# Expert weights of a mixture-of-experts trunk: loads of two units at a time, with a permuted inner index

## What is computed

```
def ffn(args):
    xb, e = args
    return (jax.nn.silu(xb @ w1[e]) * (xb @ w3[e])) @ w2[e]
```

## Time and profile before

| | |
|---|---|
| median of 3 runs | 2397.04 us (2386.5 to 2398.64) |
| the profiled execution | 2395.54 us |
| its span in the trace | 2393.7 us |
| PE busy | 2203.8 us, 92% |
| DVE busy | 1577.6 us, 66% |
| ACT busy | 1243.1 us, 52% |
| bytes moved by DMA | 598.04 MB, mean 250 GB/s |

### The profile page before, as it was taken

How to read it: one execution, slowest core, us unless ns; L and a number is a source line. 1 busy time by engine, 2 the same in 40 slices (tenths; PEclk the granted TensorE clock), 3 DMA queues, 4 the chain that set the end, 5 groups by cost and what they waited for, 6 DMA issues and landing times.

```text
span 2393.7 us, 30553 instructions
## 1 busy us (share of the span) xinstructions
PE 2203.8 (92%) x11545; PEld 1825.2 (76%) x11545; DVE 1577.6 (66%) x1338; ACT 1243.1 (52%) x1007; POOL 96.2 (4%) x74
## 2 busy tenths in 40 slices
PE   4798889999999999899897899999999999999991
PEld 3776667888999999688786777777777777777771
DVE  5433332443545455544535799999999999999996
ACT  2322223443333232233422588888888888888870
POOL 1000000000000000000100000000000000000000
PEclk9977777999999999899998799999999999999995
DMA  4411213565544444355644299999999999999983
GB/s 157 145 62 62 66 54 103 189 204 164 185 159 159 157 159 146 100 192 193 213 141 181 110 416 411 406 421 412 420 412 419 408 419 409 416 405 421 410 347 143
DMA packets 153498, 598.04 MB, mean 250 GB/s; under 512 B 15648, under 2 KB 19856, under 8 KB 102080
## 3 DMA queue, kind: packets, MB, share of 16 engines
q1 hardware_dynamic: 149760, 589.60, 64.8%
q0 software_dynamic: 3680, 7.64, 1.0%
HBM read 590.90 MB, written 18.87 MB: 255 GB/s over the span
## 4 chain that ended last, share of the span: by engine, by line
PE 72%; DVE 14%; issue 9%; ACT 2%; DMA 1%; POOL 0%; DVEq 0%; SPq 0%; ACTq 0%; POOLq 0%
PE ps L1488 19%; PE ps L1474 13%; PE ps L864 9%; DVE wl L618 8%; PE ps L865 8%; PE ps L861 5%; PE ps L845 3%; PE ps L886 2%; PE ps L1536 2%; PE ps L1557 1%; PE ps L1580 1%; PE ps L1578 1%; ACT wh L507 1%; PE ps L1548 1%; DVE yall L743 1%
## 5 line engine op out<-in xcount | busy, mean ns | idle before, releaser
L618 DVE TENSOR_TENSOR wl<-raw,wh 128x2048 fp32r<-128x2048 f32 x352 | 786.8, 2287 | 58.7 <-ACT wh L507 57.5
L507 ACT ACTIVATE wh<-raw 128x2048 fp32r<-128x2048 f32 x352 | 665.0, 1913 | 122.6 <-PE ps L865 73.4
L1168 DVE TENSOR_TENSOR wl<-raw,wh 128x2048 fp32r<-128x2048 f32 x161 | 368.9, 2292 | 498.2 <-ACT wh L1028 498.2
L1028 ACT ACTIVATE wh<-raw 128x2048 fp32r<-128x2048 f32 x161 | 308.1, 1914 | 631.9 <-PE ps L1488 301.2
L864 PE MATMUL ps<-wh,xg 128*128 128x512 f32 x900 | 383.5, 426 | 0.9 <-issue 0.7
L865 PE MATMUL ps<-wl,xg 128*128 128x512 f32 x900 | 360.6, 401 | 0.0
L1474 PE MATMUL ps<-hth,wh 128*128 128x272 f32 (+1 forms) x896 | 261.2, 291 | 15.4 <-DVE wl L1168 9.9
L1474 PE MATMUL ps<-htl,wh 128*128 128x272 f32 (+1 forms) x896 | 258.6, 289 | 0.0
L1474 PE MATMUL ps<-hth,wl 128*128 128x272 f32 (+1 forms) x896 | 258.2, 288 | 0.0
L864 PEld LDWEIGHTS ps<-wh,xg 128*128 128x128 f32 x900 | 173.9, 193 | 52.6 <-DVE wl L618 9.7
L864 PE MATMUL ps<-wh,hx 128*128 128x512 f32 x508 | 204.9, 403 | 3.4 <-DVE hx L736 3.4
(11 more groups left out here) (320 smaller groups left out, 3227.3 us busy)
## 6 DMA issues: line engine op xcount, KB each, us to landing
raw<-in_w_dram SPq DMA_DIRECT2D x384, 1024.0 KB, 8.2
raw<-in_w_in_dram SPq DMA_DIRECT2D x104, 1024.0 KB, 5.1
raw<-in_w_pa_dram SPq DMA_DIRECT2D x16, 1024.0 KB, 5.0
raw<-in_w_pb_dram SPq DMA_DIRECT2D x16, 1024.0 KB, 5.0
raw<-in_w_out_dram SPq DMA_DIRECT2D x16, 1024.0 KB, 5.1
raw<-in_w_ukv_dram SPq DMA_DIRECT2D x8, 1024.0 KB, 5.3
raw<-in_w_uq_dram SPq DMA_DIRECT2D x8, 768.0 KB, 4.5
yrow<-yscr SPq DMA_DIRECT2D x4, 1024.0 KB, 10.8
```

What stands on the lines that cost most here:

```text
L507: nc.scalar.activation(wh2[:, x % HELD, :], raw2[:, slot2(x), :], ACT.Copy).then_inc(s_wh2, 1)
L618: nc.vector.tensor_tensor(wl2[:, slot2(x), :], raw2[:, slot2(x), :], wh2[:, x % HELD, :].bitcast(F32), ALU.subtract).then_inc(s_wl2, 1)
L1028: nc.scalar.activation(wh[:, n % 2, :], raw1[:, n % RING1, :], ACT.Copy).then_inc(s_wh, 1)
L1168: nc.vector.tensor_tensor(wl[:, n % 2, :], raw1[:, n % RING1, :], wh[:, n % 2, :].bitcast(F32), ALU.subtract).then_inc(s_wl, 1)
```

## The change

Two neighbouring units, in two neighbouring slots, are loaded by one DMA of 2 MB, 16 KB in one run per partition. A matrix is two loads instead of four. A load waits until both slots are used (`x + 1 - RING2`), and both units share one semaphore, so there are four instead of eight; `hi` and `unit` wait on the semaphore of the pair of slots. `landed2` keeps its values.

`w2` is now viewed as `w1` is: partition p has the rows 4 p to 4 p + 3, and unit c has row 4 p + c. So the hidden index is permuted: the 128 hidden values of unit c are those at 4 p + c. ACT's copy to `ab` makes that order, by reading PSUM with a step of 4 elements; `mix` reads `ab[:, v, f, :]`.

```
-        ab = place("ab", [P, 2, FF], M0)
+        ab = place("ab", [P, 2, KF, P], M0)
-        s_raw2 = [sem(f"s_raw2_{i}") for i in range(RING2)]
+        s_raw2 = [sem(f"s_raw2_{i}") for i in range(RING2 // 2)]
...
                 else:
-                    done(sp, turn, x - RING2)
-                sp.dma_start(unit_view(raw2, slot2(x)) if len(src.shape) == 3 else raw2[:, slot2(x), :],
-                             src).then_inc(s_raw2[slot2(x)], 16)
+                    done(sp, turn, x + 1 - RING2)
+                s = slot2(x)
+                sp.dma_start(raw2[:, s:s + 2, :].rearrange("p s u -> p (s u)"), src).then_inc(s_raw2[s // 2], 16)
+
+            def matrix(turn, x, w, e):
+
+                v = w[bass.ds(e, 1), :, :].rearrange("a (p k) n -> p (a k n)", p=P)
+                for h in range(2):
+                    load(turn, x + 2 * h, v[:, 2 * U * h:2 * U * (h + 1)])
             def up(turn, x, w, e):
-                v = w[bass.ds(e, 1), :, :].rearrange("a (p k) n -> p (a k) n", p=P)
-                for u in range(4):
-                    load(turn, x + u, v[:, 4 * u:4 * u + 4, :])
+                matrix(turn, x, w, e)
             def down(turn, x, e):
-                for c in range(KF):
-                    load(turn, x + c, w2[bass.ds(e, 1), P * c:P * (c + 1), :].rearrange("a p n -> p (a n)"))
+                matrix(turn, x, w2, e)
...
-                act.wait_ge(s_raw2[slot2(x)], landed2(turn, x))
+                act.wait_ge(s_raw2[slot2(x) // 2], landed2(turn, x))
...
-                nc.scalar.activation(ab[:, v, :], ps[:, v, :], ACT.Copy).then_inc((s_ac, s_bc)[v], 1)
+                nc.scalar.activation(ab[:, v, :, :], ps[:, v, :].rearrange("q (p c) -> q c p", c=KF), ACT.Copy).then_inc((s_ac, s_bc)[v], 1)
...
-                    pe.wait_ge(s_raw2[slot2(x)], landed2(turn, x))
+                    pe.wait_ge(s_raw2[slot2(x) // 2], landed2(turn, x))
...
-                        nc.tensor.matmul(ps[:, 6, c:c + SLOTS], ab[:, v, P * f:P * (f + 1)], fold[:, :],
+                        nc.tensor.matmul(ps[:, 6, c:c + SLOTS], ab[:, v, f, :], fold[:, :],
```

## The result

The changed kernel takes 2460.5 us (median of 6 runs, 2453.2 to 2466.3), the kernel before 2395.2 us in the same runs: a ratio of 1.028, with a 95% interval from 1.025 to 1.031. The forecast was 2403 us, with a range from 2387 to 2420. The change is slower by 65 us, more than ten times the 6 us that the sum had.

The account below looks back on a forecast made before the run. PE was taken to bound half of each pair of experts and DVE the other half, with DMA close. 15 pairs x 0.4 us = 6 us, on top of 2397.0 us, gave 2403 us, with a range from 2387 to 2420.

Parts of the forecast that it names:

- What bounds the kernel now: Expert stage: four resources within a few per cent; PE bounds half of each pair of experts, DVE the other; 61.4 us average.
- Fewer, longer loads: Expert weight loads: 16 KB runs take 2.43 instead of 2.48 us per MB, 1.2 us of 60 per pair.
- The copy to `ab` and the order of `w2`: ACT's stepped PSUM read, 587 ns to double, taken at nothing; the hidden index's order, nothing.
- The ring in pairs: Expert-stage loads: the even unit lands 2.5 us later, costing 0.4 us per pair, with 0 and 1.2 as ends.
- I take its late landings at nothing: Half from k = 14 to k = 2: late landings cost nothing; without cover, up to the same again.
- the forecast's own sign of being wrong: The forecast is wrong if the half from k = 14 to k = 2 exceeds 29.7 us, or the `ab` copy doubles.
- The clock gives it back: Rival, expert stage: longer waits make half-clock stretches go missing, each returning 1.6 us; time 2397 us, chance 0.23.
- Late in full: Rival, expert loads: no faster runs, queue dry more often, 1.2 us per pair; 2415 us, or 2427 with half clock; chance 0.27.
- The signs named in advance: Changed profile: landings 8.5 to 11 us, ACT's DMA waits 10 to 30, `select` wait about 1.4 per pair, rate within 1%.

## Why the prediction was wrong

**What bounds the kernel now: right in the main.** DMA, PE and DVE were within six per cent of each other; ACT, at 84%, was not, though the forecast counted it with them. DVE's `select` ahead of the mix and the half clock after it were read rightly: moving `select` gave 60.8 us per pair for 61.45 and left no half-clock stretch.

**Fewer, longer loads: right in kind.** The runs take 1.3 to 2.4% less of the DMA engines' time, where the forecast had 2%. The estimate of 0.6% from the Trainium skill's cycles per packet (DMA: Bandwidth & Descriptors, Why small descriptors are slow) was too little, as far as kernels with rings of different sizes can be compared. In a ring of 8 it brings nothing; the changed kernel's queue even spent more per byte, 2.48 us per million.

**The copy to `ab` and the order of `w2`: right,** nothing (ratio 1.0003). In the changed kernel the copy takes 585 ns:

```profile
L523 ACT ACTIVATE ab<-ps 128x512 f32<-128x512 f32 x46 | 26.9, 585 | 1.1 <-PE ps L868 1.0
```

**The ring in pairs: this step failed.** The forecast had 0.4 us per pair, with 1.2 as the worst. It was 3.9. The step took the timetable of one pair of the kernel before, moved the landing of single units in it, and read off how late ACT and DVE would be. There the odd unit was to land "as before, as long as the queue has work", and the even one 2.5 us later. In the changed kernel a 2 MB load lands 9.8 us after its issue (median), where single loads of odd units took 8.0 and of even units 8.6. So the odd unit is 1.8 us later, counted from the use that lets it be asked for. The even one, asked for a unit of 2.7 us later, is 3.9 us later.

The other thing that the step missed is that the timetable itself hangs on the landings. A late copy makes a late subtraction, PE ends its unit late, and that is what the next load waits for. So a delay isn't paid once in a pair but comes round again, in both halves. The forecast's "I take its late landings at nothing" for the half that PE bounds failed with it, and it was the larger part: that half went from 29.7 to 32.0 us, the other from 31.8 to 33.4. A half longer than 29.7 us was the forecast's own sign of being wrong. That the loss is in this loop is read from the waits and the chain; the experiments show that too little lead is its cause.

What should have been done is a sum that needs no timetable. A unit takes 61.4 / 24 = 2.56 us. ACT can begin unit x when x - 4 is used. Before, the load was asked for when x - 8 was used, 4 units or 10.2 us earlier: this is the unit's lead. The median load took 8.2, which leaves 2.0 us to spare. In the changed kernel the even unit has a lead of 3 units, 7.7 us. The forecast itself named 8.5 to 11 us for the landing of 2 MB, which is 0.8 to 3.3 too much, and didn't put the two side by side. The 2.3 + 2 x 2.5 = 7.3 us of an empty queue would have given no warning, with 0.4 to spare.

The table has this sum for each kernel. The landing times are medians from 1500 to 2250 us, even and odd units apart. Where the even unit is taken only when the odd one has landed, its time runs to that landing. The next two columns are what PE did in these 750 us: how long it stood still (gaps over 0.1 us) and how long it ran at half clock.

| kernel | even unit: lead - landing = spare | odd unit | PE still | half clock | ratio |
|---|---|---|---|---|---|
| before | 10.2 - 8.6 = 1.6 | 10.2 - 8.0 = 2.2 | 12 | 24 | 1 |
| late issue alone | 7.7 - 7.4 = 0.3 | 10.2 - 9.5 = 0.7 | 18 | 14 | 1.001 |
| joint landing alone | 10.2 - 10.8 = -0.6 | 10.2 - 7.7 = 2.5 | 21 | 10 | 1.001 |
| all one unit late | 7.7 - 7.5 = 0.2 | 7.7 - 8.1 = -0.4 | 20 | 10 | 1.002 |
| both edits, 1 MB loads | 7.7 - 9.9 = -2.2 | 10.2 - 9.4 = 0.8 | 48 | 34 | 1.027 |
| changed | 7.7 - 9.8 = -2.1 | 10.2 - 9.8 = 0.4 | 49 | 24 | 1.028 |
| even two late, odd one | 5.1 - 6.9 = -1.8 | 7.7 - 8.9 = -1.2 | 48 | 70 | 1.031 |
| all two units late | 5.1 - 7.6 = -2.5 | 5.1 - 7.4 = -2.3 | 57 | 109 | 1.053 |
| 12 slots in pairs | 17.9 - 10.3 = 7.6 | 20.5 - 10.3 = 10.2 | 12 | 20 | 1.000 |

Down to 0.6 too little the loss is under 0.3%; from 1.8 too little it is 2.7% and more. The two harmless edits add up: the late issue takes 1.3 of the 1.6 us to spare, the joint landing 2.2, and with both the sum is -1.9, the measured lack 2.2. PE stands still 48 to 49 us in all three kernels whose even unit lacks 1.8 to 2.2 us. What sets the two slowest apart is in part the clock. At half clock PE loses at most half of the time: with all units two late that is up to 43 us of 750 more than before, as an estimate. How the loss follows from the lack was not worked out. Nor does the sum hold where the DMA queue is itself the bound: with `select` moved, loads land after 10.8 and 10.4 us against a lead of 10.1, and that kernel is faster than the one before.

**"The clock gives it back": it happened in the two halves of the change,** and hides most of what each costs. In the kernels with the late issue alone and with the joint landing alone ACT does wait for landings, 39 and 56 us in 750, and PE stands still 6 and 9 us longer than before. But between 1500 and 2250 us, some twelve pairs, they have three half-clock stretches each (with the late issue one is of double length), where the kernel before has seven. At 1.6 us each, 5 to 6 us in 750 come back, 0.4 to 0.5 per pair, and the times come out at 1.0006 and 1.0005. The clock could never give back 3.9 us per pair, since it costs 0.8 of one before. In the changed kernel seven stretches are left in that time. That the stretches go missing because the stop falls elsewhere is not shown; no run tried it by itself.

**"Late in full": the right rival with too small a price.** It named the queue that runs dry and the point from which it decides, 0.5 us after ACT could start; it priced one round, 1.2 us per pair, not one that comes back.

**The signs named in advance:** landing times of 8.5 to 11 us were right (median 9.8). ACT's waits for DMA were to be 10 to 30 us, and were 121. The rate was to stay within 1%, and fell by 6% (414 to 390 GB/s). PE's wait for `select` was to grow and stayed at 1.0; the new waits of PE are for subtracted weights, 33.6 us in 28 times, at other places of the pair. The packets did halve (42148 to 19850 in 750 us). The clock was no sign at all: half-clock stretches in about one pair of two were to mean the forecast, and there are seven in eleven and a half pairs.

## What to carry to other kernels

Before making loads in a ring longer, write down for the worst unit how long the ring lets it be under way, in units times their mean, and set the time to landing of the longer load against it; two edits that each fit into the same spare time may not fit together. Merging neighbours takes lead twice, once when the load is asked for and once when it is taken. And where several resources are within a few per cent of each other, look first at the small stop that holds them apart: here moving one 0.8 us step gave 12.6 us, while the 2 MB loads by themselves gave nothing even with the slots that they need.

## What the runs showed of the hardware

Loads that find the queue short cost more than their own bytes. In the changed kernel the DMA engines were busy with this queue for 95.7% of 750 us and moved 289.09 MB, 2.48 us per million bytes; with 12 slots and the same loads it was 98.3% for 307.01 MB, 2.40. The rows, the changed kernel first:

```profile
q1 hardware_dynamic: 19850, 289.09, 95.7%
```

```profile
q1 hardware_dynamic: 21090, 307.01, 98.3%
```

In the changed kernel a packet of 16 KB takes 0.611 us in the median. Of those that start 1 to 2.5 us after a load was issued, the mean is 0.759 us when the load before is less than 4 us from its landing, 0.668 with 4 to 6 us left and 0.623 with more. They hold some 26 of the 42 us by which the packets of one engine, in 750 us, exceed that median. So the forecast's fixed 2.5 us per MB holds for a full queue, and a ring that is short pays twice: for the idle time and for slower starts. Why those packets are slow stays open.

In the kernel before, TensorE's clock was at half (1.2 GHz) for 3.4 us at a time in every second pair, behind a stop of about 1 us and a mix of short matmuls; without the stop it stayed at 2.4 GHz for the 750 us. Every pair has the stop and the mix, so why it fell in every second one only stays open. So the wait of 1.0 us per pair cost up to 1.8 us with what the clock added; the 12.6 us that its removal gave are 0.8 per pair, since DMA then bounds.
